# Second block's projections as one stage of 30 split units with the convolutions between them, and the delta rule's preparation with four tiles in turn

## The reference, cut to what matters

```python
proj = x @ w_in                          # 512x1024 by 1024x7696, without the gates
(qA, kA, vA, zA, aA, bA, glu, zB, qC, kC, vC, zC,
 qD, kD, vD, zD, fD, gates) = jnp.split(proj, SPLIT_POINTS, axis=-1)
qkvA = jax.nn.silu(causal_dwconv(concat([qA, kA, vA]), conv_qkv))      # 4 taps, 1536 channels
gA = -jnp.exp(a_log) * jax.nn.softplus(aA + dt_bias); betaA = sigmoid(bA)
oA = gated_delta_rule(qA, kA, vA, gA, betaA)     # chunks of 64; solves (I + lower) for each
hB = g_lin * jax.nn.sigmoid(g_gate)
hB = causal_dwconv(hB, conv_dw) + conv_dw_bias                         # 31 taps, 512 channels
hB = jax.nn.silu(layer_norm(hB, conv_ln_g, conv_ln_b))
oC = stick_breaking_attention(qC, kC, vC)
oD = forgetting_attention(qD, kD, vD, log_sigmoid(fD + forget_bias))
```

## Time and profile before

| | us |
|---|---|
| median of 3 runs | 3535.06 |
| lowest and highest | 3530.25, 3536.33 |
| the profiled execution's own time | 3532.39 |
| its span, first to last instruction | 3530.5 |
| span of the projections' stages (737.5 to 1162.3) | 424.8 |
| span of `delta_prepare` (1324.2 to 1428.6) | 104.4 |

### The profile page before, as it was taken

One profiled execution on the slowest core, in us unless ns is written; L12 is line 12 of the kernel. 1 busy time (PEld: TensorE's weight loads), 2 busy tenths in 40 slices (PEclk: granted clock), 3 DMA queues, 4 the chain that ended last, 5 costly groups with the idle time before them and its releaser, 6 DMA issues. The chain is left out here.

```text
span 3530.5 us, 47383 instructions
## 1 busy us (share of the span) xinstructions
PE 3206.9 (91%) x17020; PEld 2513.0 (71%) x17020; DVE 2233.2 (63%) x2888; ACT 1559.1 (44%) x1959; POOL 235.1 (7%) x192
## 2 busy tenths in 40 slices
PE   7888899999997887899997977889999999999996
PEld 5756787876445556788775855668888888888884
DVE  4375776334904254545545373469989998999895
ACT  1263333011003552210114153357787778777783
POOL 0000000000000000000000000012121212121211
PEclk8889999999997897799998988979999999999998
DMA  5411222232112000022454201289999999999994
GB/s 167 160 31 37 83 95 104 82 108 76 72 48 72 25 1 2 28 98 98 149 217 176 54 7 40 72 324 381 392 378 393 376 393 376 395 376 394 377 394 163
DMA packets 159255, 636.66 MB, mean 180 GB/s; under 512 B 13457, under 2 KB 76305, under 8 KB 101922
## 3 DMA queue, kind: packets, MB, share of 16 engines
q1 hardware_dynamic: 148866, 596.63, 44.6%
q0 software_dynamic: 9648, 35.13, 3.7%
q10 hardware_dynamic: 624, 3.29, 0.2%
HBM read 604.28 MB, written 30.46 MB: 180 GB/s over the span
## 5 line engine op out<-in xcount | busy, mean ns | idle before, releaser
L518 DVE TENSOR_TENSOR experts_rest<-experts_weights,experts_leading 128x2048 fp32r<-128x2048 f32 x386 | 879.4, 2286 | 80.7 <-ACT experts_leading L3394 79.1
L3394 ACT CAST experts_leading<-experts_weights 128x2048 fp32r<-128x2048 f32 x387 | 733.1, 1917 | 27.4 <-PEq L3384 16.6
L526 PE MATMUL psum<-experts_leading,experts_xT_rest 128*128 128x512 f32 x1024 | 399.8, 390 | 0.0
L525 PE MATMUL psum<-experts_rest,experts_xT_leading 128*128 128x512 f32 x1024 | 399.6, 390 | 0.0
L524 PE MATMUL psum<-experts_leading,experts_xT_leading 128*128 128x512 f32 x1024 | 399.4, 390 | 0.0
L525 PEld LDWEIGHTS psum<-experts_rest,experts_xT_leading 128*128 128x128 f32 x1024 | 192.8, 188 | 40.9
L526 PEld LDWEIGHTS psum<-experts_leading,experts_xT_rest 128*128 128x128 f32 x1024 | 192.6, 188 | 40.3
L524 PEld LDWEIGHTS psum<-experts_leading,experts_xT_leading 128*128 128x128 f32 x1024 | 192.9, 188 | 39.3
L524 PE MATMUL psum<-experts_leading,experts_hidden_leading 128*128 128x512 f32 x512 | 205.5, 401 | 0.0
L526 PE MATMUL psum<-experts_leading,experts_hidden_rest 128*128 128x512 f32 x512 | 200.5, 392 | 0.0
L525 PE MATMUL psum<-experts_rest,experts_hidden_leading 128*128 128x512 f32 x512 | 199.6, 390 | 0.0
(11 more groups left out here) (745 smaller groups left out, 6725.1 us busy)
## 6 DMA issues: line engine op xcount, KB each, us to landing
experts_weights<-in_w_up SPq DMA_DIRECT2D x259, 1024.0 KB, 9.5
experts_weights<-in_w_down SPq DMA_DIRECT2D x128, 1024.0 KB, 6.3
ada_unit<-in_w_ada SPq DMA_DIRECT2D x12, 2048.0 KB, 16.3
merge_first<-in_w_merge SPq DMA_DIRECT2D x16, 768.0 KB, 4.1
merge_weights<-in_w_merge SPq DMA_DIRECT2D x16, 768.0 KB, 4.1
ff_up_first<-in_w_up SPq DMA_DIRECT2D x11, 1024.0 KB, 4.8
ff_up_weights<-in_w_up SPq DMA_DIRECT2D x11, 1024.0 KB, 4.8
down_first<-in_w_down SPq DMA_DIRECT2D x8, 704.0 KB, 5.0
```

The costliest lines, as they stand in the source:

```text
L518: return dve.tensor_tensor(out, src, leading.bitcast(F32), ALU.subtract)
L525: pe.matmul(out, lh, rl, start=False, stop=False)
L526: return pe.matmul(out, ll, rh, start=False, stop=stop)
L3394: act.copy(leading[h % LEADING], weights.half(h)).then_inc(masked, 1)
```

## The change

The projections become one stage. All 512-wide sections are cut in 30 units of 256 columns (1 MB each) in one array `w2`, all split, in this order: 0 to 9 the gated convolution and q, k, v of A; 10 to 15 branch D (14 and 15 by tokens); 16 to 23 the four z; 24 to 29 branch C (28 and 29 by tokens). A unit is two jobs of one PSUM bank each, in turn through three banks. The rates' columns are made first, unsplit, in their own bank, and their functions run between units. The convolutions' taps, the layer norm's steps and the Silus are placed between the units in the lists of DVE, ACT and PE. The rest of x is first kept in `y` and, once the real x is stored in DRAM (`x_kept`), moved over `k.x` from unit 10 on; `stick_breaking` loads x back. The leading part of every unit is made by ACT, the rest by DVE.

In `delta_prepare` the four tiles' decays and key products come first, then 24 steps (step s is tile s % 4 at level s // 4), with the transposes, end rows and their readers spread over the first steps, and the four tiles' last products at the end. One DVE instruction now subtracts both halves of the inverse (512 columns), and POOL sets the inverses to the identity.

SP in the projections' stage loads the units and keeps x:

```diff
+                for u in range(1, N):
+                    if u >= 2:
+                        sp.wait_ge(ready, 2 * (u - 1))
+                    sp.dma_start(ring[u % 2], k.dram["w2"][u, :, :]).then_inc(second_landed if u % 2 else first_landed, 16)
+                    if u == 1:
+                        sp.dma_start(rate_bias[:, :], k.dram["rate_biases"][0:1, :].broadcast_to([P, 2 * H + F])).then_inc(bias_landed, 16)
+                        sp.dma_start(x_kept, k.x[:, :, :].rearrange("p k t -> p (k t)")).then_inc(kept, 16)
```

PE there; `sum_stripes` is 16 matmuls of ones by the chunks' stripes, `spread_rows` 4 that spread one row to all partitions:

```diff
+                def rates_of_tokens():
+                    w = rate_weights.rearrange("p (k n) -> p k n", k=KD)
+                    pe.wait_ge(first.landed[2], 16)
+                    for t in range(TT):
+                        out = k.psum[:, 4 * BANK + t * (2 * H + F):4 * BANK + (t + 1) * (2 * H + F)]
+                        for kk in range(KD):
+                            last = pe.matmul(out, k.x[:, kk, t * P:(t + 1) * P], w[:, kk, :], start=(kk == 0), stop=(kk == KD - 1))
+                    last.then_inc(rates_ready, 1)
...
+                def job(u, j):
+                    i = 2 * u + j
+                    high, low = (x[u % 2].rearrange("p (k n) -> p k n", k=KD) for x in (leading, rest))
+                    low_source = rest_at_first if u < SWITCH else rest_later
+                    if i >= BANKS:
+                        pe.wait_ge(emptied, i - BANKS + 1)
+                    if u == 0:
+                        pe.wait_ge(split, j + 1)
+                    elif j == 0:
+                        pe.wait_ge(split, u + 2)
+                    if u == SWITCH and j == 0:
+                        pe.wait_ge(moved, KD)
+                    if by_tokens(u):
...
+                        for kk in range(KD):
+                            if i == 0:
+                                pe.wait_ge(source_split, kk + 1)
+                            last = three_passes(pe, k.bank(i % BANKS), (high[:, kk, here], low[:, kk, here]),
+                                                (lead(kk), low_source[:, kk, :]), kk == 0, kk == KD - 1)
+                    last.then_inc(ready, 1)
...
+                rates_of_tokens()
+                for u in range(N):
+                    if u == 17:
+                        pe.wait_ge(convolved, 4 * CONV_K)
+                        sum_stripes(acc, 0, added)
+                    if u == 18:
+                        pe.wait_ge(picked, 1)
+                        pe.wait_ge(averaged, 1)
+                        spread_rows(mean, 0, placed)
+                    if u == 19:
+                        pe.wait_ge(squared, len(norm_chunks))
+                        sum_stripes(squares, P, summed)
+                    if u == 20:
+                        pe.wait_ge(turned, 1)
+                        spread_rows(rstd, P, spread)
+                    for j in range(2):
+                        job(u, j)
```

ACT there (`take` copies or activates a bank's result to its place):

```diff
+                act.wait_ge(rates_ready, 1)
+                act.copy(rate[:, :, :], k.bank(4, TT * (2 * H + F)).rearrange("p (t w) -> p t w", t=TT)).then_inc(rates_taken, 1)
+                for w in range(N):
+                    if w:
+                        take(w - 1, 1)
+                    if w + 1 < N:
+                        mask(w + 1)
+                    take(w, 0)
+                    if w == 3:
+                        rate_functions()
+                    if 5 <= w < 9:
+                        move_rest(2 * (w - 5), 2 * (w - 4))
+                    if w == 17:
+                        act.wait_ge(added, 1)
+                        act.activation(mean[:, :], k.bank(3, P), ACT.Copy, scale=-1.0 / BANK).then_inc(averaged, 1)
+                    if w == 18:
+                        for n in norm_chunks:
+                            act.wait_ge(centered, n + 1)
+                            act.activation(squares[:, n, :], acc[:, n, :], ACT.Square).then_inc(squared, 1)
+                    if w == 19:
+                        act.activation(warm[:, :], k.c("one"), ACT.Sqrt).then_inc(warmed, 1)
+                        act.wait_ge(summed, 1)
```

DVE there (`long_tap` is 4 instructions, `short_tap` 12, `split_unit` the rest of one unit):

```diff
+    taps = {w: 3 if w < 15 else 1 for w in range(5, 16)}
...
+                split_first(0)
+                split_source(0, KD)
+                split_first(1)
+                tap = 0
+                for w in range(N):
+                    if w in taps:
+                        long_tap(tap)
+                        tap += 1
+                    if w + 1 < N:
+                        split_unit(w + 1)
+                    if w == 2:
+                        rates_open()
+                    if w == 4:
+                        rates_close()
+                        open_glu()
+                    for _ in range(taps.get(w, 1) - 1):
+                        long_tap(tap)
+                        tap += 1
+                    if w == 16:
+                        short_tap(0)
+                        short_tap(1)
+                    if w == 17:
+                        short_tap(2)
+                    if w == 18:
+                        dve.wait_ge(placed, 1)
+                        for n in norm_chunks:
+                            dve.tensor_tensor(striped(acc[:, n, :]), striped(acc[:, n, :]), striped(k.psum[:, 4 * BANK:8 * BANK])[:, :, 0:P],
+                                              ALU.add).then_inc(centered, 1)
+                    if w == 19:
+                        dve.wait_ge(rooted, 1)
```

SP in `stick_breaking`:

```diff
+                sp.dma_start(k.x[:, :, :].rearrange("p k t -> p (k t)"), x_kept).then_inc(x_back, 16)
```

PE in `delta_prepare`; `decay` makes a tile's two decay sums, `products` its key products, `turn_values`, `turn_keys` and `end_rows` are 4 matmuls each of 128x128:

```diff
+                def middle(s):
+                    t = s % TT
+                    pe.wait_ge(levels, s + 1)
+                    if s < TT:
+                        pe.wait_ge(begun, 1)
+                    else:
+                        pe.wait_ge(updated, s - TT + 1)
+                    if s >= 2:
+                        pe.wait_ge(copied, s - 1)
+                    for h in range(H):
+                        hc = slice(h * C, (h + 1) * C)
+                        for rows in halves:
+                            last = pe.matmul(k.bank(4 + s % 2)[rows, hc], lev[rows, t, hc], inv[rows, t, 0, hc], start=True, stop=True)
+                    last.then_inc(middles, 1)
...
+                def change(s):
+                    t = s % TT
+                    pe.wait_ge(copied, s + 1)
+                    if s < 2:
+                        pe.wait_ge(decays, s + 3)
+                    else:
+                        pe.wait_ge(updated, s - 1)
+                    for h in range(H):
+                        hc = slice(h * C, (h + 1) * C)
+                        for rows in halves:
+                            last = pe.matmul(k.bank(s % 2)[rows, hc], inv[rows, t, 1, hc], mid[rows, s % 2, hc],
...
+                for t in range(TT):
+                    decay(t)
+                    products(t)
+                middle(0)
+                for s in range(STEPS):
+                    if s + 1 < STEPS:
+                        middle(s + 1)
+                    change(s)
+                    if 1 <= s <= 3 * TT:
+                        (turn_values, turn_keys, end_rows)[(s - 1) % 3]((s - 1) // 3)
```

ACT in the steps:

```diff
+                for s in range(STEPS):
+                    act.wait_ge(middles, s + 1)
+                    if s >= 2:
+                        act.wait_ge(changes, s - 1)
+                    act.copy(mid[:, s % 2, :], k.bank(4 + s % 2, WC)).then_inc(copied, 1)
+                    t, n = (s - 4) // 3, (s - 4) % 3
+                    if 0 <= t < TT:
+                        if n == 0:
+                            weigh_keys(t, kb, 2)
+                        elif n == 1:
+                            weigh_keys(t, k_dec, 1)
+                        else:
+                            end(t)
```

DVE in the steps:

```diff
+                for s in range(STEPS):
+                    t = s % TT
+                    here_ = inv[:, t, 0:2 if s < STEPS - TT else 1, :].rearrange("p a c -> p (a c)")
+                    dve.wait_ge(changes, s + 1)
+                    if s >= TT:
+                        dve.wait_ge(updated, s - TT + 1)
+                    dve.tensor_tensor(here_, here_, k.bank(s % 2, 2 * WC if s < STEPS - TT else WC), ALU.subtract).then_inc(updated, 1)
+                    if s < STEPS - TT:
+                        level(s + TT)
+                    if s % 3 == 2 and s // 3 < TT:
+                        weigh_values(s // 3)
+                    if s % 3 == 1 and 0 <= s // 3 - 1 < TT:
+                        query_products(s // 3 - 1)
+                    if s % 3 == 2 and 0 <= s // 3 - 2 < TT:
+                        queries(s // 3 - 2)
```

More of the change, by code:

```diff
@@ new lines, in delta_rule @@
+        kb, vb = sb("kb", [P, TT, W]), sb("vb", [P, TT, W])
+        ga, dec = sb("ga", [P, TT, WC]), sb("decay", [P, TT, 2, WC])
+        lev, inv = sb("level", [P, TT, WC]), sb("inverse", [P, TT, 2, WC])
+        mid, ex = sb("middle", [P, 2, WC]), sb("ex", [P, 3, TT, H])
+        gb = answers[:, 0:TT, :]
+        LEVELS = 6
+        STEPS = TT * LEVELS
```

(43 more changed lines are left out.)

710 lines of the change are left out of this document (358 added, 352 removed).

## The result

The changed kernel takes 3413.28 us (median of 4 runs, 3411.11 to 3416.87), the kernel before 3534.47 in the same comparison: a ratio of 0.966, 95% interval 0.9643 to 0.9676. Predicted were 3422 and a range of 3408 to 3456. The profiled execution took 3416.87 (its span 3415.0, its mean clock 0.948), 115.5 less than that of before. A clock here is the granted TensorE clock in the profile (PEclk), as a share of full speed; "half clock" is a reading of 0.50.

What follows compares the result with a forecast made beforehand. PE was taken to bound the projections, except in gaps and openings, and a queue of tiles delta_prepare. 3532.4 - 73.6 (projections) - 37.6 (delta_prepare) = 3421.2 us; with the profiled execution 2.7 under the median, 3422 likeliest, range 3408 to 3456.

Steps and rivals of the forecast that it cites:

- the chain of weights: Projections: landing, leading part (ACT) and rest (DVE) of the next unit's weights take 9.6 us, within a unit's 10.88.
- Sums and spreads 4.9: Projections: the norm's sums (32 records, 1.94 us, twice) and two spreads of 8 records among the units take 4.9 us.
- Stalls 4.5: Projections: PE waits 1.6 us for unit 18's rest and 2.9 us at unit 19 for ACT's last square, together 4.5.
- The 40.0 of splitting: Projections: 28 chunks, each 1.43 us shorter when split, give 40.0 us of the gain.
- Rates, decays, products and the clock 12.1: delta_prepare's opening on PE: rates' sums 0.5 us, four tiles' decay sums and key products 7.6, half-clock loss 4.0.
- Steps with transposes and end rows 42.9: delta_prepare: 24 steps of 1.41 us, the last four shorter, take 31.9; 12 transposes or end rows take 11.0.
- Hand-overs of 2.2: delta_prepare: hand-overs at the turn into the last products cost 2.2 us.
- Rival 1: Projections: the weights' chain, not PE, is the bound; 56 us given back, total 3478 us; chance 0.07.
- rival 3: Whole kernel slower than before, through the chain of weights in 28 units; 3559 us at an 11 us landing; chance 0.02.
- Rival 2: delta_prepare: steps don't fill PE, or the clock stays low; 3450 us, or 3480 if all; chance 0.10.
- rival 4: Projections: DVE is late in the ten rounds of taps, +4 us, within the likeliest case; no separate chance given.
- the +2.3 for POOL first: delta_prepare: if POOL's identity copy precedes DVE's first mask, PE's first decay sum waits, +2.3 us; 0 was taken.

Runs made afterwards that it cites:

- the best version: Changed kernel with short taps spread, norm centering earlier, and two unread matmuls filling the gap before the scan: 3400.69 us, ratio 0.963; second time 3400.86 us, 0.9627.

## Why the prediction was right

The projections were priced at 351.2 and took 350.4. Term by term:
- Rates 10.1, measured 10.1 (735.5 to 745.6). The first unit's loss at half clock 1.7, measured 2.2 (745.63 to 758.73, less 10.88). Both terms have chance in them: in two other executions they took 1.6 us more together.
- A unit at 10.88 and one by tokens at 11.56: measured 10.88 and 11.51. That the chain of weights fits under a unit is shown by the waits: none of PE but the two at units 18 and 19. Its 9.6 were 9.05.
- Sums and spreads 4.9, measured 1.1 + 0.5 + 1.2 + 0.5 and small gaps, about 4. The 32 records of a sum took 1.08 where the earlier trace rows has 1.94 at a clock of 0.50.
- Stalls 4.5: the places were right, the sizes 0.8 and 1.9. DVE's first 12 short taps took 0.41 each and not 0.47, the others 0.66 for 0.69.
- Missing from the sum: 1.7 of half clock behind the second stall. It made up for most of the stalls' error; that the total came within 0.8 us is partly luck.
- The 40.0 of splitting is shown (22.8 for 16 chunks, so 1.42 each). That both the store of x and its way back are hidden is seen from PE having no wait for them. They landed after 11.0 and 8.6 us by the DMA issues.

`delta_prepare` was priced at 66.8 and took 63.9:
- Rates, decays, products and the clock 12.1 together, measured 11.6 (1247.24 to 1258.86), again by two errors against each other: a tile's decays and products took 2.32 at full clock where 1.9 was reckoned (1.7 for the four), and half clock cost about 1.8 instead of 4.0, since it was over some 4 us after the start and not 8.
- Steps with transposes and end rows 42.9, measured 43.0, but by two errors against each other. The transposes were priced as 8 records for four of them, and have 4: 8 x (0.92 - 0.59) = 2.6 too much. End rows took 1.09 for 0.92, and each piece of side work about 0.14 more than its own time, some 2.4 us together.
- Last products 8.3, measured 8.3 (to 1310.1). Start, end and meeting 1.3, measured 1.0.
- Hand-overs of 2.2 at the turn into the last products: none. With the errors above largely set against each other, this term is most of the 2.9.

In the steps one transpose took 0.147 us (0.59 / 4), an fp32 matmul of the same shape 0.27 (1.09 / 4).

By the rows the gain of 40.6 is 25.3 of PE's idle time (26.3 before, 1.0 after) and 15.3 of its busy time, for nearly as many records (1496 and 1484) at a clock of 0.97 instead of 0.82. Among the waits of before are the 9.0 us for `delta_gb` that the prediction named, and as many as 8.3 for `delta_level`, which it did not name:

```profile
PE psum L1940 <- DVE delta_level L2055: 8.3, 2, 4.2
```

Both are gone. By the runs four in turn is 6.8, the merged subtraction nothing with four in turn; what the preparation ahead of all steps gave, and what the clock, was not divided by a run.

Rival 1 was wrong for this kernel and right about the danger: with 5.44 us more in the chain the change loses all. Its slope, however, was too low, and so was rival 3's: they let a late load cost only the wait. The waits of 3.6 us cost 2.0 more in the mean, by the clock, so a late load is some 1.5 times as dear. Rival 2 didn't happen; the steps fill PE. Nor did rival 4: the taps stood 0.69 apart, and PE had no wait in units 5 to 14. POOL's copy of the identity and DVE's masks ran together, 2.01 us and 3.02 for the pair, and PE had no wait: the 0 was right. DVE was the first of the two in all eleven profiles of the new `delta_prepare`, by some 0.2 us, so no run shows the +2.3 for POOL first.

The total was 8.7 us lower than predicted: 4.3 from the profiled execution (0.8 and 3.0 in the two parts, 0.5 elsewhere), 3.6 since this execution was the slowest of its four, and 0.8 that the prediction had added because that of before was under its median. That the stages outside the two parts came out at 0.5 is luck: the scan's +6.3 stands against -6.8 of the others, and no term had either.

## What to carry to other kernels

Where one engine is busy nearly all the time, price the change as that engine's stream, instruction by instruction, and then look for each place where its input is ready later than the stream arrives; the stages came out within 1% and 5% in this way. An idle time of PE near 2 us or more should be priced above its own length, for the clock: here 1.93 us cost 1.7 more, and waits of 3.6 us 2.0 more in the mean, though not each time. Look at the first matmul behind each meeting of the engines in a stage of small matmuls: two matmuls that nothing reads gave more there (7 to 19 us) than a re-ordering did in the projections (4.4), and a profile of one execution can mislead, since that stage's length varied by 12 us between executions of one kernel.

## What the runs showed that was not expected

- After idle times of 0.3, 0.66 and 0.82 us PE kept its full clock, and after the 1.5 among the last products of the kernel before; after 1.93 and most of those near 3.7 in the dense stream it went to 0.50 for some 3 to 4 us. At the scan 1.94 us of idle time were followed by some 17 to 44 us at 0.50, with PE busy in 86 to 90% of the stage by its records (36.0 of 41.9 us, 48.4 of 53.8).
- The scan took 53.8 or 41.9 to 42.0 us in eight executions with the new `delta_prepare` and the gap as it was, four times each, 47.5 and 43.1 with the old one, and 34.5 to 35.0 in four executions of three kernels with the gap filled. The two executions of the changed kernel (53.8 at a mean clock of 0.55, 41.9 at 0.78) show that the time at the lower clock varies; on what it depends no run here shows. Why the scan takes so long to get its clock back, and why there are two lengths, is open.
- Gains of 4 to 19 us in one stage were in part lost again in later stages of the profiled executions (4.9 to 0.1 in one, 18.8 to 10.0 in another), in code that is the same. Below some 5 us a stage's own time was the sharper measure, though it too moved by up to 2 us; the whole told the best version from the changed kernel only in runs of both on one chip.
